# First block's MLP: one 512-column product for both activation halves in the up stages, the row scale moved to the down stages

## What is computed

```python
def _rmsnorm(x, g):
    xf = x.astype(jnp.float32)
    y = xf * lax.rsqrt(jnp.mean(xf * xf, axis=-1, keepdims=True) + EPS)
    return (y * g.astype(jnp.float32)).astype(x.dtype)

def _sq_relu_mlp(h, w_up, w_down):
    u = jax.nn.relu(h @ w_up)
    return (u * u) @ w_down

# in both layers of the first block
x = x + _sq_relu_mlp(_rmsnorm(x, a_norm_mlp[i]), a_w_up[i], a_w_down[i])
```

## Time and profile before

| | us |
|---|---|
| median of 3 runs | 1170.97 |
| lowest and highest run | 1170.64, 1171.49 |
| span of the profiled execution | 1169.1 |
| PE busy in the span | 1150.3 |
| DVE busy in the span | 887.9 |
| ACT busy in the span | 752.0 |
| POOL busy in the span | 326.2 |

### The profile page before, as it was taken

The page is one execution under the profiler, slowest core; times in us unless marked ns, Lnnn a source line. Parts: engine busy times, 40 slices in busy tenths (PEclk is TensorE's granted clock), DMA queues, the critical chain, the costliest instruction groups (busy, mean ns, idle before and its releaser), DMA issues.

```text
span 1169.1 us, 25942 instructions
## 1 busy us (share of the span) xinstructions
PE 1150.3 (98%) x8640; PEld 1069.5 (91%) x8640; DVE 887.9 (76%) x1510; ACT 752.0 (64%) x1373; POOL 326.2 (28%) x297
## 2 busy tenths in 40 slices
PE   9999999999999999999999999999999999999998
PEld 8988999999898999999898789999889988999987
DVE  7888877666578867766659978988556776899954
ACT  7766655445566655545467878887456666887842
POOL 3220355300012245532302105555000310444400
PEclk9999999999999999999999999999999999999999
DMA  8654565666655465666653345655745744565672
GB/s 321 197 151 144 169 198 199 197 198 197 216 161 159 137 201 194 206 207 207 210 175 127 126 152 195 208 190 202 218 148 183 242 137 139 186 198 193 202 221 103
DMA packets 64055, 216.62 MB, mean 185 GB/s; under 512 B 7777, under 2 KB 10993, under 8 KB 63985
## 3 DMA queue, kind: packets, MB, share of 16 engines
q1 hardware_dynamic: 63808, 215.17, 56.4%
q10 hardware_dynamic: 176, 0.54, 0.2%
HBM read 211.47 MB, written 1.06 MB: 182 GB/s over the span
## 4 chain that ended last, share of the span: by engine, by line
PE 83%; DVE 9%; ACT 3%; issue 2%; DMA 1%; POOL 1%; SPq 0%; DVEq 0%; POOLq 0%; ACTq 0%
PE bank L821 11%; PE bank L823 11%; PE bank L822 11%; PE bank L819 9%; PE bank L816 5%; PE bank L739 4%; PE bank L741 4%; PE bank L740 4%; PE bank L688 4%; PE bank L690 3%; PE bank L689 3%; DVE w_lo L1648 3%; PE bank L617 2%; PE bank L618 1%; PE bank L623 1%
## 5 line engine op out<-in xcount | busy, mean ns | idle before, releaser
L1648 DVE TENSOR_TENSOR w_lo<-raw,w_hi 128x1024 fp32r<-128x1024 f32 x386 | 506.4, 1322 | 69.2 <-ACT w_hi L1182 68.8
L1182 ACT CAST w_hi<-raw 128x1024 fp32r<-128x1024 f32 x386 | 401.8, 1047 | 214.7 <-PE bank L823 49.4
L821 PE MATMUL bank<-h_hi,w_hi 128*128 128x256 f32 x1184 | 327.6, 277 | 0.4
L822 PE MATMUL bank<-h_lo,w_hi 128*128 128x256 f32 x1184 | 325.6, 275 | 0.0
L823 PE MATMUL bank<-h_hi,w_lo 128*128 128x256 f32 x1184 | 325.6, 275 | 0.0
L821 PEld LDWEIGHTS bank<-h_hi,w_hi 128*128 128x128 f32 x1184 | 227.2, 192 | 2.0 <-DVE h_lo L1730 1.2
L822 PEld LDWEIGHTS bank<-h_lo,w_hi 128*128 128x128 f32 x1184 | 227.3, 192 | 0.1
L823 PEld LDWEIGHTS bank<-h_hi,w_lo 128*128 128x128 f32 x1184 | 227.3, 192 | 0.0
L819 PE MATMUL bank<-a,w_hi 128*128 128x512 f32 x496 | 163.3, 382 | 0.0
L688 PE MATMUL bank<-h_hi,w_hi 128*128 128x256 f32 x512 | 144.6, 282 | 0.3 <-ACT v_tok L1429 0.3
L689 PE MATMUL bank<-h_lo,w_hi 128*128 128x256 f32 x512 | 140.8, 275 | 0.0
(11 more groups left out here) (234 smaller groups left out, 2059.6 us busy)
## 6 DMA issues: line engine op xcount, KB each, us to landing
raw<-in_w_up_sb SPq DMA_DIRECT2D x44, 512.0 KB, 3.5
raw<-in_w_up_fox SPq DMA_DIRECT2D x44, 512.0 KB, 3.5
raw<-in_w_up_a SPq DMA_DIRECT2D x32, 512.0 KB, 3.4
raw<-in_w_down_a SPq DMA_DIRECT2D x32, 512.0 KB, 4.6
raw<-in_w_up_b SPq DMA_DIRECT2D x32, 512.0 KB, 4.3
raw<-in_w_down_b SPq DMA_DIRECT2D x32, 512.0 KB, 5.3
raw<-in_w_in_sb SPq DMA_DIRECT2D x24, 512.0 KB, 3.6
raw<-in_w_in_fox SPq DMA_DIRECT2D x24, 512.0 KB, 4.2
```

The costliest lines, as they stand in the source:

```text
L821: nc.tensor.matmul(dst, w_hi[:, slot, w], in_turns(src_hi[:, at + k, :]), start=begin, stop=False)
L822: nc.tensor.matmul(dst, w_hi[:, slot, w], in_turns(src_lo[:, at + k, :]), start=False, stop=False)
L1182: nc.scalar.copy(w_hi[:, slot, 0:k * P], raw[:, slot, 0:k * P]).then_inc(hi_ready, 1)
L1648: nc.vector.tensor_tensor(w_lo[:, slot, 0:k * P], raw[:, slot, 0:k * P], w_hi[:, slot, 0:k * P].bitcast(f32), ALU.subtract).then_inc(lo_re ...
```

## The change

- **Up stages a and b** join `WIDE`: `h2_hi` and `h2_lo` become the two halves of one tensor `h2`, and a K tile takes one 512-column product (w_hi with both halves) and one of 256 columns (w_lo with the high half). The high and the low result now lie side by side in the bank.
- **Their eviction** is one `tensor_reduce` over the 512 columns that adds each pair of halves (`both_products`), with neither ReLU nor scale, and no wait for `rstd`.
- **ReLU** becomes an operation of its own on ACT, in place on `u_buf`, ahead of ACT's square. POOL waits for it (`relu_ready`) where it waited for `tile_out`.
- **The first trip** no longer holds back the tiles of these stages. `norm_scale` still follows the second tile; for `up_a` and `up_b` it raises the mean square to -1 instead of -0.5, which is the squared row scale.
- **Down stages a and b**: the eviction becomes three operations on DVE, one `tensor_reduce` of the bank into a new buffer `y_down`, one multiplication by `rstd`, one addition to X.

```diff
...
-        h2_hi = sb("h2_hi", [P, KT, TOK], f32r)
-        h2_lo = sb("h2_lo", [P, KT, TOK], f32r)
+        h2 = sb("h2", [P, 2, KT, TOK], f32r)
+        h2_hi, h2_lo = h2[:, 0], h2[:, 1]
...
+        y_down = sb("y_down", [P, TOK])
...
-        WIDE = {"down_a": 0, "down_b": D // P}
+        WIDE = {"up_a": h2, "down_a": a, "up_b": h2, "down_b": a}
+        UNSCALED = ("up_a", "up_b")
+        SUMS = {"down_a": 0, "down_b": 2 * D // P}
...
+        def both_products(b):
+
+            return bank[b][:].rearrange("p (s a h) -> p h a s", s=2, h=2)
...
                             if name in WIDE:
-                                both, pair = bank[b][:], high_and_low(a, at + k)
+                                both, pair = bank[b][:], high_and_low(WIDE[name], at + k)
...
-                    holds = first and name in MS_AFTER and s <= MS_AFTER[name]
+                    holds = first and name in MS_AFTER and s <= MS_AFTER[name] and name not in UNSCALED
...
+                    if first and s == MS_AFTER.get(name) and middle is not None:
+                        middle()
                     if holds and s == MS_AFTER[name]:
-                        if middle is not None:
-                            middle()
...
                     act.wait_ge(tile_out, i * 4 + (first_tile + b + 1))
+                    nc.scalar.activation(u_buf[:, b, :], u_buf[:, b, :], ACT.Relu).then_inc(relu_ready, 1)
+                    act.wait_ge(relu_ready, i * 4 + (base + b + 1))
                     nc.scalar.activation(a_hi[:, i * 4 + b, :], u_buf[:, b, :], ACT.Square).then_inc(a_hi_ready, 1)
...
-                nc.scalar.activation(dst[:], log_ms[:], ACT.Exp, scale=-0.5).then_inc(rstd_ready, 1)
+                power = -1.0 if list(NORMS)[n_norm[0]] in UNSCALED else -0.5
+                nc.scalar.activation(dst[:], log_ms[:], ACT.Exp, scale=power).then_inc(rstd_ready, 1)
...
                     dve.wait_ge(units_done, done)
-                    x = halves_of(X[:, i * per + b, :])
-                    nc.vector.tensor_tensor(x, product(b), x, ALU.add).then_inc(high_added, 1)
-                    dve.wait_ge(high_added, i * per + (WIDE[name] + b + 1))
-                    nc.vector.tensor_tensor(x, low_product(b), x, ALU.add).then_inc(tile_out, 1)
+                    dve.wait_ge(rstd_ready, NORMS[DOWN_OF[name]] + 1)
+                    x, at = X[:, i * per + b, :], i * (2 * per) + (SUMS[name] + 2 * b)
+                    nc.vector.tensor_reduce(halves_of(y_down[:]), both_products(b), AX.X,
+                                            ALU.add).then_inc(halves_joined, 1)
+                    dve.wait_ge(halves_joined, at + 1)
+                    nc.vector.tensor_tensor(y_down[:], y_down[:], rstd[:], ALU.mult).then_inc(halves_joined, 1)
+                    dve.wait_ge(halves_joined, at + 2)
+                    nc.vector.tensor_tensor(x, y_down[:], x, ALU.add).then_inc(tile_out, 1)
...
                     dve.wait_ge(units_done, done)
-                    dve.wait_ge(rstd_ready, NORMS[name] + 1)
                     dve.wait_ge(a_ready, i * 4 + (base + b + 1))
-                    nc.vector.scalar_tensor_tensor(halves_of(u_buf[:, b, :]), product(b), 0.0, halves_of(rstd[:]),
-                                                   ALU.max, ALU.mult).then_inc(tile_out, 1)
+                    nc.vector.tensor_reduce(halves_of(u_buf[:, b, :]), both_products(b), AX.X,
+                                            ALU.add).then_inc(tile_out, 1)
...
                     for b in range(4):
-                        pool.wait_ge(tile_out, i * 4 + (first_tile + b + 1))
+                        pool.wait_ge(relu_ready, i * 4 + (base + b + 1))
...
```

More of the change, by code:

```diff
@@ L303, in build_program @@
         gain_joined = sem("gain_joined")
-        high_added = sem("high_added")
+        halves_joined = sem("halves_joined")
+        relu_ready = sem("relu_ready")
         mem_added = sem("mem_added")
@@ L2243, in relu @@
             def relu(name):
-                base, first_tile = PRODUCTS[name], plan[name]["tile"]
+                base = PRODUCTS[name]
                 with pool.Fori(0, plan[name]["trips"]) as i:
                     for b in range(4):
-                        pool.wait_ge(tile_out, i * 4 + (first_tile + b + 1))
+                        pool.wait_ge(relu_ready, i * 4 + (base + b + 1))
                         pool.wait_ge(a_ready, i * 4 + (base + b + RING - 1))
```

## The result

| | before | after |
|---|---|---|
| median of 4 runs, us | 1171.23 | 1182.68 |
| lowest and highest | 1170.64, 1172.17 | 1182.02, 1183.76 |
| span of the profiled execution | 1169.1 | 1180.2 |

The ratio is 1.010, with a 95% interval of 1.0088 to 1.0112: slower by about 1.0%, 11.5 us. The forecast was slower at 1179.8 us with a range of 1171.5 to 1191.0. The sign, the mechanism in the up stages and most of the size held; 3.3 us in the down stages were missed.

What follows compares the result with a forecast made beforehand. PE was taken to bound the kernel, with DVE close behind. up_a +2.6, up_b +4.7 and down-stage ends +1.5 gave +8.8 us on the 1169.1 span; with 1.9 more for the median, 1179.8 us, range 1171.5 to 1191.

Steps and rivals of the forecast that it cites:

- DVE's loop is what PE's gain runs into: Up stages: DVE's lengthened step exceeds PE's 2.62 us a tile, so PE's saving of at most 3.8 us is lost.
- The reduction costs 0.685 us: Up eviction on DVE: reading 512 columns takes 0.685 us, or +0.265 a tile.
- The scan's pace, the upper bound: Up eviction: at two steps an element, 512 elements would take about 1.17 us, total about 1211 us.
- POOL's product hides the ReLU: Up stages: POOL's product is held until DVE's split ends, so the ReLU costs DVE's loop nothing; uncovered, up to 0.55 us.
- up_a, +2.6: First up stage: PE's first down product starts at 222.6 instead of 219.99, a loss of 2.6 us.
- up_b, +4.7: Second up stage: it ends at 494.4 instead of 489.70, a loss of 4.7 us.
- The ends of the down stages, 2 x 0.73: Value stages wait uncovered for the last down tile, whose eviction grows by 0.73 us: 1.5 us in all.
- Inside a stage this is covered: Within down stages the eviction's +0.73 us costs nothing: PE has 5.2 us of weights, DVE's split ends some 4 us after the tile.
- the dearer reduction: Rival for the evictions: a reduction of 0.95 us gives 1196.8 us, at the scan's 1.17 us about 1211; chance 0.12.
- the free product: Rival in up stages: POOL's product runs free of DVE's split, giving 1168.7 us; chance 0.10, shared with a cheap reduction.
- No change: Rival: a reduction of 0.55 us gives +0.2, 1171.2 us; chance 0.10, including the remainder for PE keeping its old pace.
- That PE would not speed up: Rival in up stages: PE keeps 0.335 us a K tile, total hardly different; chance within the 0.10 for no change.

Runs made afterwards that it cites:

- Experiment 9: Changed kernel with five more, already fulfilled waits on DVE right ahead of up_b: 1181.50 us.
- experiments 1: Changed kernel whose up eviction copies only the first 256 columns, the h_lo product being ignored: 1171.42 us, ratio 0.9996.
- 2: Changed kernel with DVE forming a_lo one tile later in up_a and up_b: 1171.08 us, ratio 0.9997.
- 10: Kernel before with the 512-column product in the up stages, its h_lo product unread and the eviction as before: 1168.07 us, ratio 0.9974.
- 12: Changed kernel with a_lo one tile later (up), weight split ahead of low parts (down), value stage gated on the last down reduction: 1165.95 us, ratio 0.9954.

## Why the prediction was right, and where it was not

1. **DVE's loop is what PE's gain runs into.** Right, and shown from both sides: a shorter reduction or a better order brings back PE's pace. PE's gaps in the loop end with DVE's w_lo, as written; the idle PE before each down stage was 1.24 us and not 1.5.
2. **The reduction costs 0.685 us.** Right: 684 ns. The scan's pace, the upper bound, did not apply. The estimate worked out from the Trainium skill, 658 ns by the VectorE: DVE Perf Modes page, section "The TRN2 errata", was too low for this form.
3. **POOL's product hides the ReLU.** Right: 1.00 us long, ending 0.47 behind the split, as written; no effect without the ReLU.
4. **up_a, +2.6.** Right in sum, by luck: two errors cancel. The first eviction came 4.94 us behind PE's first product (137.02 - 132.08), not 4.54, because the split ahead of it took 1.76 us where I assumed 1.2; POOL's addition of squares ran beside it. Against that the loop's step averaged (215.91 - 147.76) / 24 = 2.84, not 2.86 us, which is 0.5 over 24 tiles.
5. **up_b, +4.7: measured +5.3.** The same long split gives 0.4. The step averaged (494.24 - 423.24) / 24 = 2.96 and not 2.945 us, 0.3 more. Experiment 9 shows that these steps change by as much with idle instructions ahead of the loop, which no row of before could tell.
6. **The ends of the down stages, 2 x 0.73.** Right. PE's idle time ahead of each value stage rose by 0.72 us (1.05 - 0.33).
7. **The step that failed: "Inside a stage this is covered".** I set 5.2 us of cover against a split that ends "some 4 us after the tile". Each figure was rounded to the kind side. Before the change the split ended 4.36 us after the tile's first operation (from 241.27 to 243.87 + 1.76), with POOL's addition already holding it, as this row of DVE before shows:

```profile
243.87 1.76 DVE L1648 TENSOR_TENSOR w_lo<-raw,w_hi 128x1024 fp32r<-128x1024 f32 x1
```

   The chain grew by 0.93, not 0.73: in the loop 0.16 us pass between the multiplication and the addition, where I had 0.04, and the rest lies in the steps behind. That gives 248.97 - 243.68 = 5.29 us. PE asked for the weights at 248.72, 5.04 us after the same operation, not 5.2. So a margin that I put at about half a microsecond was -0.25. In down_a that cost 2.5 us. In down_b most tiles kept their cover, and the one with the further split on DVE, which the forecast did not look at, cost 0.6.

Of the 12.6 us in the four stages the forecast had 8.8; the missed cover is 3.1, up_b's size 0.6, and 0.1 in each down stage is the slower restart of its first product behind the wait. The 1.5 us less outside brought the time nearer to the forecast than its parts were, which is luck.

The rivals: the dearer reduction and the free product fell with points 2 and 3. "No change" needed a reduction of 0.55 us. That PE would not speed up was wrong too: where PE sets the pace, in experiments 1, 2, 10 and 12, up_a takes 85.5 us instead of 87.3.

## What to carry to other kernels

Where the busiest engine has another one right behind it, price a change by the second engine's loop, and ask of each wait in that loop whether it is work or order: here 0.6 us of waiting in each step could be moved away, which took the change from 1% slower to even (ratio 0.9997), and the two further cures made it 0.46% faster than the kernel before. A cover has to be worked out from row to row, with the lengths that instructions have at that very place, and to a tenth of a microsecond; "5.2 against some 4" was not an argument once 0.73 was to be added. After an edit that lengthens a chain, look at the steps that other engines already lengthen, since the two add up.

## What was new about the hardware

- A two-input DVE operation is held by POOL as POOL is held by it. The split takes 1.76 us beside a POOL addition that began 0.27 us earlier, and a_lo 0.83 instead of 0.43 us beside POOL's product.
- The first product behind a gap costs PE a further 0.11 us: 0.22 to the next start instead of 0.11.
- Five already fulfilled waits ahead of a loop made the stage 1.05 us shorter, 0.09% of the time, with no work changed. Of a difference of the 0.2% that a measurement can tell here, half can come from that alone.
